# Pointwise convolution of a Hymba-style encoder layer as Strassen's seven half-size products instead of eight full-width steps

## The reference

```python
xn = rms_norm(x, pre_g)
u = einsum('btd,de->bte', xn, w_in)                   # 1024 x 5120
xr, gr, cv_v, cv_g, gc = split(u, 5)
xr = causal_dwconv(xr, 4 taps);  hr = rg_lru(xr)      # gates a, x; scan over tokens
y_r = hr * silu(gr)
v = causal_dwconv(cv_v * sigmoid(cv_g), 31 taps)
v = silu(layer_norm(v))
y_c = (einsum('btc,ce->bte', v, cv_w2) + cv_b2) * silu(gc)   # pointwise convolution, 1024 x 1024
y = einsum('btm,md->btd', concat([y_r, y_c]), w_out)  # 2048 x 1024
return x + rms_norm(y, post_g), and the states
```

## Time and profile before

| | us |
|---|---|
| median of 3 runs (lowest, highest) | 793.64 (793.53, 794.07) |
| profiled execution, its time | 792.8 |
| profiled execution, its span in the trace | 791.0 |
| PE busy in the span | 779.7 (99%) |
| DVE busy | 642.4 (81%) |
| ACT busy | 422.0 (53%) |
| POOL busy | 360.2 (46%) |

### The profile page before, as it was taken

One profiled execution on the slowest core, in us unless ns is written; L12 is line 12 of the kernel. 1 busy time (PEld: TensorE's weight loads), 2 busy tenths in 40 slices (PEclk: granted clock), 3 DMA queues, 4 the chain that ended last, 5 costly groups with the idle time before them and its releaser, 6 DMA issues. The chain is left out here.

```text
span 791.0 us, 12769 instructions
## 1 busy us (share of the span) xinstructions
PE 779.7 (99%) x5206; PEld 765.0 (97%) x5206; DVE 642.4 (81%) x562; ACT 422.0 (53%) x663; POOL 360.2 (46%) x220
## 2 busy tenths in 40 slices
PE   8999999999999999999999999999999999999996
PEld 7999999999999999999999999999999999999995
DVE  6789999999998976986995997984247987797674
ACT  6621366356347448348248369963505434576652
POOL 5424536538547557556556755000014982491000
PEclk9999999999999999999999999999999999999998
DMA  8311232272571661651521220215249232534363
GB/s 278 95 55 54 80 108 80 86 182 81 134 186 53 160 167 58 147 133 53 107 81 38 69 81 27 111 55 161 81 169 303 84 107 82 160 107 154 92 216 114
DMA packets 101164, 90.76 MB, mean 115 GB/s; under 512 B 3179, under 2 KB 85099, under 8 KB 101122
## 3 DMA queue, kind: packets, MB, share of 16 engines
q1 hardware_dynamic: 93792, 72.30, 29.4%
q0 software_dynamic: 7328, 17.90, 10.1%
q10 hardware_dynamic: 2, 0.00, 0.0%
HBM read 76.94 MB, written 30.03 MB: 135 GB/s over the span
## 5 line engine op out<-in xcount | busy, mean ns | idle before, releaser
L955 PE MATMUL ps<-act_hi,w_hi 128*128 128x352 f32 (+5 forms) x1392 | 444.9, 320 | 0.2
L957 PE MATMUL ps<-act_hi,w_lo 128*128 128x352 f32 (+5 forms) x1392 | 439.4, 316 | 0.0
L956 PE MATMUL ps<-act_lo,w_hi 128*128 128x352 f32 (+4 forms) x1328 | 421.5, 317 | 0.0
L1971 DVE SCALAR_TENSOR_TENSOR ps<-cv_in,par_cv,ps 128x1086 f32<-128x1086 f32 x232 | 313.8, 1353 | 7.8
L955 PEld LDWEIGHTS ps<-act_hi,w_hi 128*128 128x128 f32 x1392 | 261.3, 188 | 5.3 <-issue 4.5
L957 PEld LDWEIGHTS ps<-act_hi,w_lo 128*128 128x128 f32 x1392 | 261.9, 188 | 0.0
L956 PEld LDWEIGHTS ps<-act_lo,w_hi 128*128 128x128 f32 x1328 | 249.7, 188 | 0.2
L738 POOL TENSOR_TENSOR w_lo<-wstage,w_hi 128x1024 fp32r<-128x1024 f32 x40 | 97.3, 2441 | 69.6 <-ACT w_hi L1342 69.5
L956 PE MATMUL ps<-act_hi,w_hi 128*128 128x264 f32 (+2 forms) x256 | 73.0, 285 | 0.0
L1342 ACT ACTIVATE w_hi<-wstage 128x1024 fp32r<-128x1024 f32 x46 | 47.6, 1052 | 24.8 <-PE ps L957 17.7
L955 PE MATMUL ps<-act_lo,w_hi 128*128 128x264 f32 x192 | 55.4, 289 | 0.0
(11 more groups left out here) (246 smaller groups left out, 1002.4 us busy)
## 6 DMA issues: line engine op xcount, KB each, us to landing
wstage<-in_w_in SPq DMA_DIRECT2D x40, 512.0 KB, 3.9
w_sums<-in_w_out POOLq DMA_DIRECT2D x16, 1024.0 KB, 8.7
silu_spill<-silu_gc SPq DMA_DIRECT2D x8, 528.0 KB, 2.7
yr_spill<-y_rg SPq DMA_DIRECT2D x8, 528.0 KB, 4.9
silu_l<-silu_spill SPq DMA_DIRECT2D x8, 528.0 KB, 3.7
yr<-yr_spill SPq DMA_DIRECT2D x2, 2112.0 KB, 11.3
wstage<-in_cv_w_pw SPq DMA_DIRECT2D x8, 512.0 KB, 5.0
wstage<-w_sums SPq DMA_DIRECT2D x8, 512.0 KB, 5.6
```

The costliest lines, as they stand in the source:

```text
L955: pe.matmul(out, wh, xh, start=start, stop=False)
L956: pe.matmul(out, wh, xl, start=False, stop=False)
L957: return pe.matmul(out, wl, xh, start=False, stop=stop)
L1971: STT(out=acc, in0=src, scalar=w, in1=acc, op0=ALU.mult, op1=ALU.add).then_inc(taps, 1)
```

## The change

The 8 full-width steps become 28 half-size steps: the 1024 x 1024 weight is seen as 2 x 2 blocks, the tokens as two halves of 528, and seven products of sums give the four result quarters. A step t (product m = t // 4, output tile e = t % 4) is 4 tiles k x 2 chunks of 264 tokens x 3 matmuls = 24 matmuls. A weight block of 512 KB now serves two steps (14 blocks instead of 8, rows of 1 KB instead of 512 bytes). Four of the seven weight sums are made in HBM beside those of the output projection (8 more DMAs of 1 MB from POOL, in the first 4 of the 8 places, now two parts in a place); the one difference (product 3) is subtracted by POOL. POOL also makes the 20 operand sums of products 2 to 6, and multiplies 12 of the 16 result quarters' tiles by the gate; DVE does the other 4. ACT copies the results of products 0 and 1 from PSUM (with the bias, two copies for each step), DVE adds those of products 2 to 6 (two additions for each step, one in products 5 and 6). The three gate chunk pairs now stand after steps 5, 7 and 9, the turning of the states after step 20, `y_part` of the last tile moves from POOL to DVE, and the first product of the output projection takes its operands in the order 4 to 7, 0 to 3.

The core of the diff (the waits of moved lines and some helpers are left out):

```diff
-PW_BANK = [2, 5]
+PW_PRODUCTS = [((1, 0), ALU.add, (1, 1)), ((0, 0), ALU.add, (0, 1)), ((0, 0), None, None),
+               ((0, 0), ALU.subtract, (1, 1)), ((1, 1), None, None), ((1, 0), ALU.add, (0, 0)),
+               ((0, 1), ALU.add, (1, 1))]
+PW_GATES = {5: 0, 7: 1, 9: 2}
+PW_TURN = 20
+V_ORDER = [(K, k, h) for K, h in ((0, 0), (1, 1), (0, 1), (1, 0)) for k in range(QT)]
+def pw_bank(t):
+    return (2, 4, 6, 0)[t] if t < 4 else 2 + 2 * ((t - 4) % 3)
...
@@ SP
+            for q in range(4):
+                load_silu(q)
+            for u in range(2, 12):
+                load_pw(u)                       # u >= 2 waits late_los >= u - 1
+                if u // 2 == PW_SUB:
+                    load_second(u)
...
+            spill_y(KT - 1)
+            load_pw(PW_W - 2)
...
+            load_yr(1)
+            load_pw(PW_W - 1)
+            for q in range(4, 8):
+                load_silu(q)                     # q >= 4 waits yc >= q - 3
+            load_yr(0)
+            load_out(0)
+            load_out(1)
+            for q in range(8, 16):
+                load_silu(q)
@@ POOL
+            v_sums(2)
+            pw_weight_sum(2 * PW_SUB)
+            v_sums(3)
+            pw_weight_sum(2 * PW_SUB + 1)
+            v_sums(4)
+            v_sums(5)
+            for q in range(4):
+                gated(q, 2, 4 * QT)
+            v_sums(6)
+            pool.wait_ge(st_rows, 2)
...                                              # 6 state outputs
+            for q in range(4, 8):
+                gated(q, 4, 5 * QT)
+            for q in range(8, 12):
+                gated(q, 5, 5 * QT)
@@ PE
+            def pw_bank_free(t):
+                if t < 3:
+                    pe.wait_ge((ln_rstd, gc_read, gr_read)[t], (3, 2 * KT, 2 * KT + 1)[t])
+                elif t > 3:
+                    u = t - 4 if t < 7 else t - 3
+                    if u < PW_COPIED * QT:
+                        pe.wait_ge(pw_copied, 2 * u + 2)
+                    else:
+                        pe.wait_ge(pw_added, pw_adds(u))
...
+                    if e == 0:
+                        pe.wait_ge(v_lo, QT * m + k + 1)
+                    mm = pw_step(t, k)
@@ ACT
+            for k in range(1, QT):
+                normed_high(0, k)
             pw_weight(2)
+            for k in range(QT):
+                normed_silu(QT + k)
+                normed_high(1, k)
+            for t in range(PW_STEPS - QT):
+                m, e = divmod(t, QT)
+                if m < PW_COPIED:
+                    first_into(t)
+                if t == 3:
+                    for i in range(2 * QT, 3 * QT):
+                        normed_silu(i)
+                if t in (5, 6):
+                    normed_silu(2 * t + 2)
+                    normed_silu(2 * t + 3)
+                if 1 <= m < len(PW_PRODUCTS) - 1 and e < 2:
+                    normed_high(m + 1, 2 * e)
+                    normed_high(m + 1, 2 * e + 1)
+                if t in PW_GATES:
...                                              # tanh of gate chunk pair PW_GATES[t]
+                if t % 2 == 1 and t // 2 + 3 < PW_W:
+                    pw_weight(t // 2 + 3)
+                if t == 9:
+                    decay(c, 1, False)
+                if t == 12:
+                    root(c)
@@ DVE
+            for t in range(QT, PW_STEPS - QT):
+                m, e = divmod(t, QT)
+                if m >= PW_COPIED:
+                    add_into(t)
+                if m < len(PW_PRODUCTS) - 1 and e in (1, 2):
+                    pw_low(m + 1, 2 * e - 2)
+                    pw_low(m + 1, 2 * e - 1)
+                if t % 2 == 1 and t // 2 + 3 < PW_W:
+                    pw_weight_low(t // 2 + 3)
+                if t == 11:
                     ix_part(c)
+                if t == 12:
                     q_part(c)
+                if t == 13:
                     b_part(c)
                     scan(c, 1)
                     save_h(c)
+                    y_part(c, 2 * KT + 1)
...
+            for ei in range(QT):
+                t = PW_STEPS - QT + ei
+                add_into(t)
+                gated(PW_STEPS - QT - 12 + ei, len(PW_PRODUCTS) - 1)
+                if ei < 2:
+                    operand_low(0, 2 * ei)
+                    operand_low(0, 2 * ei + 1)
+                if ei == 1:
+                    out_low(0)
+                if ei == 2:
+                    for n in range(QT, KT - 1):
+                        operand_low(0, n)
             operand_low(0, KT - 1)
             out_low(1)
```

More of the change, by code:

```diff
@@ L466, in build @@
         st_out = sem("st_out")
-        silu_loaded = [sem("silu_loaded0"), sem("silu_loaded1")]
+        silu_loaded = [sem(f"silu_loaded{i}") for i in range(4)]
+        v_sum = sem("v_sum")
+        pw_copied = sem("pw_copied")
+        pw_added = sem("pw_added")
+        w_second = sem("w_second")
+        w_subbed = sem("w_subbed")
+        yc_v = sem("yc_v")
         pw = sem("pw")
@@ L797, in sum_part @@
             def sum_part(j):
-                q, r = j // 2, j % 2 * (KT * P // 2)
+                if j < len(PW_PRESUMMED):
+                    first, _, second = PW_PRODUCTS[PW_PRESUMMED[j]]
+                    rows = cv_w_pw2.rearrange("d n e -> (d n) e")
+                    return pw_sums[j], [rows[K * QT * P:(K + 1) * QT * P, E * QT * P:(E + 1) * QT * P]
+                                        for E, K in (first, second)]
+                q, half = divmod(j - len(PW_PRESUMMED), 2)
+                r = half * (KT * P // 2)
                 first, _, second = PRODUCTS[PRESUMMED[q]]
@@ L1810, in _ @@
             act.wait_ge(yr_in[1], 16)
+            for k in FIRST_ORDER[0:QT]:
+                operand_high(0, k)
             out_high(0)
-            for k in range(KT):
+            for k in FIRST_ORDER[QT:KT]:
                 operand_high(0, k)
@@ L2131, in _ @@
+            for i in range(QT):
+                normed(i)
+            pw_weight_low(1)
+            pw_low(0, 0)
+            for i in range(QT, 2 * QT):
+                normed(i)
+            for k in range(1, QT):
+                pw_low(0, k)
             for k in range(1, RW):
                 rtap(c, 1, k)
-            w_lo_part(2, 0, N_PW + 3)
-            def pw_out(k):
-                h = k % 2
-                dve.wait_ge(pw, k + 1)
-                dve.wait_ge(silu_loaded[h], k // 2 * 16 + 16)
-                STT(out=conv_out[:, k:k + 1, 0:TO].rearrange("p a (j n) -> p (a j) n", j=3),
-                    in0=ps[:, PW_BANK[h]:PW_BANK[h] + 3, 0:OCH], scalar=par[:, k, P_B2:P_B2 + 1],
-                    in1=silu_l[:, h].rearrange("p (j n) -> p j n", j=3), op0=ALU.add,
-                    op1=ALU.mult).then_inc(yc, 1)
@@ L2145, in _ @@
-            pw_out(0)
+            pw_weight_low(2)
+            for k in range(QT):
+                pw_low(1, k)
+                if k % 2 == 1:
+                    for i in range(2 * QT + k - 1, 2 * QT + k + 1):
+                        normed(i)
             dve.wait_ge(rtaps, 3 * c + 3)
```

373 lines of the change are left out of this document (224 added, 149 removed).

## The result

The changed kernel takes **818.70 us** (median of 5 runs, 817.75 to 819.10), the kernel before beside it 793.53. The ratio is 1.031, with a 95% interval of 1.030 to 1.033: slower by 25.2 us. The prediction was 816.0 with a range of 797 to 828. The profiled execution took 819.0, its span is 817.1: 26.1 us more than before.

A forecast was written before the change was run, and what follows sets the result against it. PE's list of matmuls was taken to bound the kernel; -10.7 + 4.1 + 3.7 + 6.0 + 13.3 + 4.8 + 1.2 = +22.4 on the profiled 792.8 gave 815.2, as a median 816.0 us, range 797 to 828.

The forecast's parts named there:

- PE's own work: PE's matmul list in the changed stage: 86.2 us against 96.9, so 10.7 us less if PE never waits.
- First wait: PE at step 4 waits for ACT's copies of step 0, behind weight block 2: 4.1 us (3 to 6).
- Second wait: PE at gate pair 1 waits for ACT to free pair 0's banks: 3.7 us (2 to 5).
- Third wait: Products 2 and 3: DVE's SBUF instructions take turns with POOL and PE waits 6.0 us (0 to 10).
- the rival at 791: ACT's late start is the only wait and DVE catches up meanwhile: 791 us, down to 783; chance 0.12.
- Fourth wait: Product 4: low parts of tiles 2 and 3 stand behind the last RG-LRU tile in DVE's queue: 13.3 us.
- Fifth wait: Output projection's start: POOL sends states before its last 8 gatings, so gate loads come late; 4.8 us with smaller waits.
- The clock, 1.2: PE working at a lower clock behind the wait in product 4: 1.2 us added to the sum.
- the rival at 827: Weight blocks land a us later, yr 3 us later, the clock falls three times: +11 more, 827 us; chance 0.10.
- What costs nothing: POOL's 8 more DMAs in the loop, about 9 us of its time, hide in its idle time.
- DVE and POOL: Sign: DVE's 528 column subtractions with a mean near 1.2 us instead of 0.7, POOL's near 1.6.
- The other side (791): The same case as the rival at 791; it decides if all waits together stay under 10.7 us.

The follow-up runs named there:

- Run 1: The changed kernel with weight block 2's high part (ACT) and low part (DVE) moved behind product 1's SiLUs and operand parts: 815.65 us.
- Run 6: The changed kernel with POOL starting product 5's sums and the first gatings only once product 4's low parts are done: 814.50 us.
- Runs 2 and 3: Changed kernel with product 4's four low parts ahead of the last RG-LRU tile: 818.38 us; the same with that tile cut over steps 13 to 15: 818.06 us.
- run 4: The changed kernel with POOL issuing the 6 state outputs behind its last gatings: 818.87 us.
- run 5: The changed kernel with POOL's state outputs sent last and SP's gate loads 8 to 15 ahead of the output projection's second weight load: 815.42 us.
- run 7: The changed kernel with 54 unread filler matmuls on PE ahead of tile 2 of step 16: 817.76 us (with 90: 824.03 us).
- run 8: The kernel before with only the four more weight sums made in HBM, read by nobody: 793.53 us against 793.43.

## Why the prediction was right

The forecast fell 2.7 us short, and two of its terms were wrong by more than that, in opposite directions. The direction and the longest wait came by the mechanism named; that the number came so near is in part luck.

- **PE's own work, -10.7.** Right. From the end of the turning at 604.7 to the output projection's wait at 625.4 are 7 steps, 2.96 us each (predicted 2.94); the whole account, with the clock's 10.6 as estimated from the windows, closes within 0.4 us.
- **First wait, 4.1.** Measured 4.8. ACT's copies come at 524.25, behind weight block 2 (landed 516.6, predicted 516.9) and product 1's SiLUs. Run 1 confirms the place of the block.
- **Second wait, 3.7.** Measured 3.2, at the gate pair and for ACT.
- **Third wait, 6.0: the mis-sized step.** Products 2 and 3 show no wait; one of 0.7 stands ahead of tile 1 of product 4. Turns between DVE and POOL do take place in products 2 and 3 (two low parts in 2.46 at 559.54), but I had added them in full to the first two waits. Those two made PE 8.0 us late, then it ran at a granted clock of 0.50 from 543 to 549, and DVE used that time, as the rival at 791 had said of it. In run 1, where PE came 3.5 us sooner to product 2, a wait of 0.9 stands there; the rest stayed covered.
- **Fourth wait, 13.3.** Measured 13.4, by the mechanism named. Run 6 splits it: 7.3 without POOL beside it. Two figures of the working don't follow from its terms: 2.8 + 20.3 + 0.1 - 10.3 is 12.9 and not 13.3, and without the turns 2.8 + 13.5 + 0.1 - 10.3 is 6.1, where the text has 7.9 "without POOL's turns and their backlog". So 7.3 is near the 7.9, but the 7.9 isn't worked out. Runs 2 and 3 show that it isn't only the low parts: the bank releases stand behind the same tile.
- **Fifth wait, 4.8.** Measured 3.8, all of it at step 0; the size was near, the cause half of it. "POOL sends them and only then makes its last 8 gatings" is what held the gate loads in the changed kernel (614.65, behind the gating of 613.29), but a second cause stood right behind it, SP's weight load ahead of them in the queue (613.18 in run 4). Taking away the first alone gained nothing (run 4); with the second gone as well, 3.5 us (run 5).
- **The clock, 1.2: mis-sized.** The 1.2 in the sum is my estimate for PE's work at a lower clock behind the wait in product 4, and no run shows it; the windows of the changed kernel give 10.6 by the estimate above, 3.0 of it behind that wait (2.6 in run 7). I had priced one long wait. All four long waits, the ones of 3.2 to 4.8 us too, were followed by 3 to 6 us at the lower level (the windows at 0.50 to 0.81 above). Little of it was covered by the next wait: where run 7 gave PE 2.6 us back, that wait grew by 0.3. That the clock falls several times was in the prediction only as a part of the rival at 827; the other part of that rival, later transfers, did not come (block 2 landed at 516.6).
- **What costs nothing.** The HBM sums: confirmed by run 8.
- **DVE and POOL.** DVE's 20 subtractions from the sums average 1.14 us (predicted near 1.2), POOL's sums 1.93 (predicted near 1.6), as POOL waits for DVE too:

```profile
L1005 POOL TENSOR_TENSOR act_x<-conv_out 128x528 f32<-128x528 f32 x20 | 37.9, 1925 | 21.8 <-PE ps L1092 20.4
```

The terms add up to -10.7 + 25.9 + 10.6 instead of -10.7 + 31.9 + 1.2. Six us too much for waits and nine too little for the clock gave a good sum by luck; the clock term alone would have made it 825.

The other side (791) needed all waits together under 10.7. With three of the causes repaired they are still 18.2, and no order that I ran came under 808. Whether a version under 793.5 exists, with fewer operations of DVE and POOL in the stage, stays open; it wasn't tried.

## What to carry to other kernels

Half-size products save a sure share of PE's list (here 10.7 of 96.9 us) and ask the elementwise engines for operand sums, split parts and additions in each product. Before making such a change, add up the busy time of each engine in the stage: here DVE went from 53 to 95 us for a PE list of 86. Better orders of the queues took back 10.6 of the 25 us, and three orders then ended at 808 to 809, still 15 above the kernel before. Price each of PE's waits twice, once for itself and once for the stretch at the lower clock behind it (here 1.7 to 3.1 us by the estimate, behind waits of 3.2 to 13.4); and where a wait has been removed, look for who arrives sooner and what it then waits for, before counting the gain. A repair that gains nothing can still be right: the sends of POOL had to go before the order of SP's loads could pay.

## What was unexpected of the hardware

- A wait of 3.2 us of PE at a gate pair was followed by a granted clock of 0.50 until about 549, 3.1 us lost by the estimate from the windows: as much as behind the 13.4 us wait (3.0). Waits of 1.64 (run 1) and 1.1 (run 5) left the granted clock at 1.00.
- DVE's instructions with two operands in SBUF took longer beside POOL even where they are tiny: the scan of 32 columns took 1.25 us instead of 0.26, the product of 32 columns 1.28 instead of 0.18, about 1 us more as for the scan of 1040 columns (3.30 instead of 2.32). In these rows the cost goes by the instruction and not by its size. DVE's 32 additions from PSUM took 0.70 on average, 0.69 to 0.71.
- A float32 matmul of 128 columns from float32 operands took 0.222 us in a row of them, in two records each, against 0.14 for one of the prologue's transposes (8 in 1.10 us).
